# GpSimd's queue in the expert loop of a hybrid decoder block: scatter and both gathers ahead of the power

## The reference

```python
x = x + hybrid_mixer(rms_norm(x, mix_norm_w), ...)
x = x + memory_cross_attention(rms_norm(x, xattn_norm_w), ...)
x = x + hierarchical_moe(rms_norm(x, ffn_norm_w), ...)   # 32 experts, 2 for each token
return rms_norm(x, final_norm_w)

def hierarchical_moe(...):          # the top group of 4, then the top 2 of its 8 experts
    for e in range(N_EXPERTS):
        hid = jax.nn.silu(t @ w_gate[e]) * (t @ w_up[e])      # 1024 -> 256
        y = y + gates[:, e:e + 1] * (hid @ w_down[e])         # 256 -> 1024
```

## Time and profile before

| what | value |
|---|---|
| median of 3 runs (lowest, highest) | 1997.42 us (1981.85, 1997.9) |
| the profiled execution, its own time | 1975.81 us |
| its span on core 6, the slowest | 1972.6 us |
| spans of the other cores | 1944.7 to 1967.7 us |
| mean granted TensorE clock of core 6 | 0.871 |
| busy, share of the span: TensorE, VectorE, ScalarE, GpSimd | 72%, 68%, 47%, 47% |
| the last stage on core 6 | about 1423 to 1966 us |

### The profile page before, as it was taken

One profiled execution on the slowest core, in us unless ns is written; L12 is line 12 of the kernel. 1 busy time (PEld: TensorE's weight loads), 2 busy tenths in 40 slices (PEclk: granted clock), 3 DMA queues, 4 the chain that ended last, 5 costly groups with the idle time before them and its releaser, 6 DMA issues.

```text
span 1972.6 us, 27269 instructions; the slowest of 8 cores (1944.7 to 1972.6 us)
## 1 busy us (share of the span) xinstructions
PE 1421.4 (72%) x7761; PEld 670.3 (34%) x7904; DVE 1339.4 (68%) x2214; ACT 935.0 (47%) x1771; POOL 928.5 (47%) x1078
## 2 busy tenths in 40 slices
PE   3787877878889788862577676777178867777786
PEld 1443433444444344331233332333033322323332
DVE  4688688888687778771465847686347656666676
ACT  4455555564645555540536364553035434444444
POOL 2265465576473655561001111021547766666676
PEclk9888888988899899986788888897579888888899
DMA  8655646455757464657235271322275767777762
GB/s 215 212 129 121 142 100 129 107 139 121 152 118 155 104 136 90 113 126 160 104 107 182 70 208 38 124 96 86 74 258 166 240 233 265 256 259 257 271 207 93
DMA packets 92880, 303.82 MB, mean 154 GB/s; under 512 B 21401, under 2 KB 22553, under 8 KB 89280
## 3 DMA queue, kind: packets, MB, share of 16 engines
q0 software_dynamic: 49312, 137.59, 29.6%
q1 hardware_dynamic: 43424, 164.42, 25.9%
HBM read 396.16 MB, written 138.02 MB: 271 GB/s over the span
## 4 chain that ended last, share of the span: by engine, by line
DVE 26%; PE 23%; POOL 17%; issue 15%; ACT 10%; DMA 8%; SPq 1%; DVEq 0%; POOLq 0%; ACTq 0%
PE pst L392 21%; DVE arena L368 10%; ACT arena L365 8%; POOL arena L368 6%; DVE arena L379 6%; POOL arena L1573 5%; DVE arena L409 4%; DVE arena L372 4%; POOL out L1580 3%; PE pst L403 2%; DMA arena<-x2scr 2%; DMA arena<-x 2%; DMA out<-arena 2%; ACT arena L384 1%; POOL arena L1564 1%
## 5 line engine op out<-in xcount | busy, mean ns | idle before, releaser
L392 PE MATMUL pst<-arena 128*128 128x512 bf16 (+9 forms) x5618 | 1247.8, 361 | 321.5 <-DVE arena L368 116.6
L392 PEld LDWEIGHTS pst<-arena 128*128 128x128 bf16 (+3 forms) x5761 | 505.5, 107 | 996.6 <-issue 477.9
L365 ACT ACTIVATE arena<-arena 128x1 f32<-128x1 f32 (+9 forms) x579 | 388.8, 694 | 423.6 <-DVE arena L379 217.4
L368 POOL TENSOR_TENSOR arena<-arena 128x1 f32<-128x1 f32 (+6 forms) x389 | 403.3, 1046 | 338.0 <-DVE arena L368 180.8
L365 ACT ACTIVATE arena<-pst 128x512 bf16<-128x512 f32 (+4 forms) x549 | 290.2, 549 | 322.2 <-PE pst L392 261.4
L403 PE MATMUL pst<-arena 128*128 128x128 bf16 (+2 forms) x2143 | 220.7, 251 | 218.5 <-ACT arena L365 112.0
L368 DVE TENSOR_TENSOR arena<-pst,arena 128x512 f32<-128x512 f32 (+7 forms) x498 | 250.0, 519 | 157.2 <-PE pst L392 101.8
L379 DVE SCALAR_TENSOR_TENSOR arena<-arena 128x512 f32<-128x512 f32 (+6 forms) x361 | 337.0, 938 | 23.6 <-ACT arena L365 13.6
L384 ACT ACTIVATE arena<-pst 128x1024 bf16<-128x1024 bf16 (+4 forms) x294 | 204.4, 729 | 256.5 <-PE pst L403 181.1
L403 PEld LDWEIGHTS pst<-arena 128*128 128x128 bf16 (+2 forms) x2143 | 173.8, 116 | 294.1 <-ACT arena L365 124.5
L1408 POOL DMA_INDIRECT slots<-arena x64 | 63.8, 997 | 423.3 <-DVE arena L386 334.9
(11 more groups left out here) (22 smaller groups left out, 296.4 us busy)
## 6 DMA issues: line engine op xcount, KB each, us to landing
arena<-wbscr SPq DMA_DIRECT2D x90, 1536.0 KB, 11.8
wbscr<-we POOLq DMA_DIRECT2D x96, 512.0 KB, 6.5
arena<-x SPq DMA_DIRECT2D x64, 512.0 KB, 6.8
x2scr<-arena SPq DMA_DIRECT2D x32, 512.0 KB, 3.8
arena<-x2scr SPq DMA_DIRECT2D x32, 512.0 KB, 8.5
out<-arena SPq DMA_DIRECT2D x32, 512.0 KB, 3.2
xnscr<-arena SPq DMA_DIRECT2D x32, 256.0 KB, 2.7
arena<-wbscr SPq DMA_DIRECT2D x15, 512.0 KB, 6.3
```

The lines of the kernel that those rows point to most:

```text
L365: S.op("act", lambda e: e.activation(out=out, in_=in_, func=func, **kw), R, W, cost=c)
L368: S.op(eng, lambda e: e.tensor_tensor(out=out, in0=in0, in1=in1, op=op), R, W, cost=ecost(eng, out))
L392: i = e.matmul(o, lhsT=l, rhs=r, start=st, stop=sp)
```

## The change

Before, in the turn of t, GpSimd gets `gather(t+4)`, `zscat(t-2)`, the power of t-1, `zgather(t+1)`. After, it gets `zscat(t-2)`, `zgather(t+1)`, `gather(t+4)`, the power of t-1. In TensorE's queue the read of the next tile's ring address moves from just ahead of `gU(t+1)` to just ahead of `hTr(t)`. Up to two such addresses are then held in registers, so the set of registers kept alive grows.

```diff
+    def wreg(t):
+        SOI[t] = nc.next_id()
+        SO[t] = vload("pe", 1, t, (NRING - 1) * 6144)
+
     def gU(t):
         pb, kb = bank(2 + t % 2)
-        i0 = nc.next_id()
-        SO[t] = vload("pe", 1, t, (NRING - 1) * 6144)
+        i0 = SOI.pop(t)
         keep.clear()
-        keep.add(SO[t].val.handles[0].name)
+        keep.update(SO[u].val.handles[0].name for u in SO)
...
+    wreg(0)
     gU(0)
...
             if t + 2 < NT:
                 tT(t + 2)
-            if t + NXG < NT:
-                gather(t + NXG)
+            if t + 1 < NT:
+                wreg(t + 1)
             hTr(t)
             if t + 2 < NT:
                 tTe(t + 2)
         if t >= 2:
             zscat(t - 2)
+        if t + 1 < NT:
+            zgather(t + 1)
+        if t + NXG < NT:
+            gather(t + NXG)
         if t >= 1 and t - 1 < NT:
             sq(t - 1)
             fin1(t - 1)
         if t + 1 < NT:
             gU(t + 1)
             hid(t + 1)
-            zgather(t + 1)
         if t >= 1 and t - 1 < NT:
             fin2(t - 1)
         if t < NT:
             dN(t)
```

More of the change, by code:

```diff
@@ L1601, in wkeys @@
         return ["Wc%d" % (t % NRING)] + (["Wp%d" % t] if t < NRING else [])
+    SOI = {}
+    def wreg(t):
+        SOI[t] = nc.next_id()
+        SO[t] = vload("pe", 1, t, (NRING - 1) * 6144)
     def gU(t):
         pb, kb = bank(2 + t % 2)
-        i0 = nc.next_id()
-        SO[t] = vload("pe", 1, t, (NRING - 1) * 6144)
+        i0 = SOI.pop(t)
         keep.clear()
-        keep.add(SO[t].val.handles[0].name)
+        keep.update(SO[u].val.handles[0].name for u in SO)
         mm([(pb, xgT[t % NXT][:, kc, :], WRf[:, bass.ds(SO[t] + kc * 512, 512)], kc == 0, kc == 7) for kc in range(8)],
```

## The result

The changed kernel is slower: 2089.62 us median of four runs (2066.13 to 2113.47) against 1991.22 us for the kernel before. The ratio is 1.040, with a 95% interval of 1.029 to 1.051. The prediction said 2089. The four runs lie in two pairs, 2066 and 2069, 2110 and 2113, and the median falls between them. The profiled execution took 2066.13 us, with a span of 2063.0 on core 6, the slowest there too; before it was 1975.81 and 1972.6. The predicted span was 2065.

What follows compares the result with a forecast made beforehand. A VectorE and ScalarE ring of 5.46 us a turn bounds the kernel, with 47.6 us of disturbances. After: 81 gaps of 7.11 us, plus 3, minus 489.9, plus 3 at the start, +92: 1997.4 to 2089 us, range 2045 to 2120.

Steps and rivals of the forecast that it cites:

- the 21.6 us that were added for the median: Whole time: the median of the runs before lay 21.6 us above the profiled execution, giving 1997.4 + 92 = 2089 us.
- The ring: Last stage: power, select, `ot`, scatter, `zgather`, gather, next power close a loop through GpSimd, 7.11 us against 5.46.
- wake-up of the scatter: GpSimd, from the end of `ot` to the scatter's start: taken as 0.79 us, the unknown of the sum.
- The other end: Low bound for the scatter's start: 0.05 us, from the routing's indirect DMA woken by VectorE, without bounds check.
- The blocked gather: GpSimd's gather falls into VectorE's row scale and is held, ending near 7.08 us and not 6.68.
- The 47.6 us of disturbances: Last stage before: time beyond 81 turns of 5.46 us, mostly 44.3 us of waits for `zgather`; 3 left after.
- the late gather: Gather issued later against TensorE's use of its rows; priced at 0 to 10 us, taken within the 3.
- The start: First gaps of the last stage: the power of tile 2 stands behind the late `zgather(4)`, +3 us.
- TensorE's address read: TensorE, ahead of gU before: 0.25 us of issue; moving it gives 0 us, as TensorE isn't on the ring.
- the low clock level: TensorE at 0.85 granted over the disturbed stretch: a turn of 6.4 us, still under 7.11.
- The rival on the other side: Faster: GpSimd's ring doesn't bind, turn stays 5.46, waits for `zgather` go; -48 us, 1950 us, chance 0.03.
- point of decision: Last stage: a ring of 6.05 us a turn, under which the changed kernel would be faster than before.

Runs made afterwards that it cites:

- e1: Kernel before with only GpSimd's new order, TensorE's address read left where it was; ratio to before 1.045.
- e5: Changed kernel with five buffers for the gathered rows in place of four; ratio to before 1.048.
- e3: Changed kernel with the power written to a column nobody reads, so `ot` no longer waits for it; ratio to before 1.019.
- e4: Kernel before with GpSimd order power, gather, scatter, zgather, so the gather fills the wait for `ot`; ratio to before 1.001.
- e7: Changed kernel with VectorE's row scale made ahead of the adds, out of the gather's way; 2046.83 us, ratio to before 1.030.
- e6: e3 with five buffers for the gathered rows in place of four; ratio to before 0.999.

## Why the prediction was right

**The number.** That the median met 2089 within a microsecond is luck: no run lies within 19 us of it, and the 21.6 us that were added for the median came from other runs. What the working forecast is the profiled execution, 2068 us and a span of 2065, and it took 2066.13 and 2063.0. The ratios of e1 and e5, 1.045 and 1.048, lie at the forecast 4.7%; the one of the changed kernel, from two runs, is 1.040.

**The ring.** Predicted 7.11 us a turn, measured 7.07. Piece by piece, predicted and measured: power to select 0.61 and 0.62; select to `ot` 0.31 and 0.31; `ot` 1.28 and 1.29; wake-up of the scatter 0.79 and 0.83; scatter to `zgather` 1.31 and 1.35; `zgather` to gather 1.36 and 1.31; gather to power 1.45 and 1.36. The unknown piece, the wake-up, was taken from a `zgather` woken by a DMA, and holds for a scatter woken by VectorE. The other end, 0.05, was that of a DMA of another form. That the ring carries the loss is shown from three sides: cut, it gives back 61.5 us (e3); one DMA shorter, 87 (e4); without the row scale's hold on the gather, 23 (e7).

**The blocked gather.** Predicted to end 0.9 behind the row scale; it ended 0.87 behind (2017.00 and 2016.13). With the row scale moved, it took 1.00. This is the rule of the Trainium skill (SBUF — State Buffer, Who interferes with whom), by which the second of the two blocks until the first ends. The rows of the changed kernel and of e7 agree with it to 0.13 us.

**What comes back.** The 47.6 us of disturbances were to shrink to 3, with 0 to 10 for the late gather. They are 6.8, and 5.4 of the stage go with a fifth buffer, so the late gather is most of what is left and inside the bound. The start was priced at +3 us and was 0: 26.6 us both times. Over 81 turns the ring was 3 us shorter than forecast and the disturbances 4 us longer, so the small misses nearly cancel.

**TensorE's address read.** Priced at nothing; the stage with it alone is 1.1 us shorter and the stage without it 1.3 us shorter, so it is nothing within what two profiles can tell. The 0.25 us that the prediction read in one turn was small for the stage: there it is 49.1 us over 91 times, 0.54 each. The prediction also calls 0.85 the low clock level; it is a mean between the two levels (0.5 and 1.0 of 2.4 GHz), and the 7 us around that gU (1606 to 1613) have 0.64. The floor of some 600 ns that the Trainium skill gives such a load (DMA: Bandwidth & Descriptors, Latency and other measured facts) is near the 0.54, but shows nowhere in the time, for the bound isn't TensorE.

**The rival on the other side** was mis-sized, though it wasn't the case that came. It promised 48 us, to 1950, if the ring did not bind, from a point of decision at 6.05 us a turn. With the ring cut and a turn of 5.58, well under that point, the kernel was 1.9% slower than before, and with the gather's lateness repaired it was level (e3, e6). The step that failed is that the waits for `zgather` are lost time that a longer distance saves. With the late gather repaired, VectorE still waited 46 us for `zgather` and GpSimd 64 for scatters: the waits are one side of a loop of four tiles through two landings, and shortening one wait lengthened the other.

## What to carry to other kernels

When instructions in one engine's queue are reordered, follow each one's input back to the same queue: here the scatter needed a result that VectorE makes from the power directly ahead of it, and the two gathers that had covered that time were put behind it. Price the new ring by rows of the same instruction in the same situation, woken or not, alone or beside VectorE. And a wait for a landing is not a gain to be had until the loop that holds its other end has been added up.

## What the runs showed of the hardware

An indirect DMA with a bounds check starts 0.83 us behind the result it waited for, where one without a check had 0.05; that the check is what makes the difference was not tried. Issued behind another such DMA with nothing to wait for, it starts 0.30 to 0.31 behind that one's end.

VectorE's row scale and `ot` hold a GpSimd DMA that starts inside them: it ended 0.9 us behind their end, at a length of 1.16 (in `ot`), 1.33 and 1.54 us (in the row scale), where it takes 1.0 otherwise. They hold the power too: 0.58 us alone, 0.78 when it starts inside the row scale (e4), and 1.08 in e3, where it starts inside `ot` (1964.33, `ot` from 1963.71 to 1964.99).

A conditional load of SyncE with three register reads costs its queue 2.1 us, which limits how finely weights can be cut. The kernel before gives the same: 480 us less 316.3 of waiting, over 78 loads.
